# First mixer of a hybrid trunk on one Trainium2 core: S5 input and q/k products moved ahead of the output-gate tiles, pole exponentials packed, S5 output turned and transposed on TensorE, GLU first

## The reference, cut to what matters

```python
proj = xn @ w_in
u, xm, v, o_pre = jnp.split(proj, [512, 1024, 1536], axis=-1)
# S5: 32 groups x 16 channels, 64 complex states each
a_bar = jnp.exp(lam * dt)
b_bar = ((a_bar - 1.0) / lam)[..., None] * b
_, states = lax.associative_scan(_linear_recurrence_combine, (a_seq, bu), axis=1)
y = Re(C . states) + d_skip * u
g = jax.nn.gelu(y)
y_a = g * jax.nn.sigmoid(g @ w_glu)
# mLSTM: 4 heads of 128
xc = jax.nn.silu(causal_dwconv(xm, ml_conv_w, ml_conv_b))
q, k = per-head xc @ ml_w_q, xc @ ml_w_k
gates = concat(q, k, v) @ ml_w_gates + ml_b_gates
h_t = rmsnorm(mlstm_chunkwise(q, k, v, gates[..., :4], gates[..., 4:]))
y_b = jax.nn.sigmoid(o_pre) * h_t
return jnp.concatenate([y_a, y_b], axis=-1) @ w_out
```

## Time and profile before

| | us |
|---|---|
| median of 3 runs | 1192.64 (1188.93 to 1192.95) |
| the profiled execution, its own time | 1190.42 |
| its span, first to last instruction | 1188.2 |
| PE / DVE / ACT / POOL busy in the span | 1135.7 / 670.0 / 471.6 / 237.5 |
| mean granted TensorE clock | 0.971 |

### The profile page before, as it was taken

One profiled execution on the slowest core, in us unless ns is written; L12 is line 12 of the kernel. 1 busy time (PEld: TensorE's weight loads), 2 busy tenths in 40 slices (PEclk: granted clock), 3 DMA queues, 4 the chain that ended last, 5 costly groups with the idle time before them and its releaser, 6 DMA issues.

```text
span 1188.2 us, 15399 instructions
## 1 busy us (share of the span) xinstructions
PE 1135.7 (96%) x5386; PEld 909.4 (77%) x5386; DVE 670.0 (56%) x882; ACT 471.6 (40%) x675; POOL 237.5 (20%) x405
## 2 busy tenths in 40 slices
PE   8988779999999999999999999999999999999995
PEld 6876454877788888888888777777888888888883
DVE  5766765344766666664333566547666666652223
ACT  6324125353544344443222255535443443432221
POOL 8899797002000000000000012111000000000001
PEclk8999958899999999999999999999999999999998
DMA  6633001143223232323333321123323232223321
GB/s 225 128 105 105 1 1 58 36 142 106 88 90 106 88 104 90 105 89 106 106 101 102 104 75 54 38 71 107 106 88 106 88 106 88 98 97 107 106 71 71
DMA packets 39096, 108.77 MB, mean 92 GB/s; under 512 B 11984, under 2 KB 12240, under 8 KB 38928
## 3 DMA queue, kind: packets, MB, share of 16 engines
q1 hardware_dynamic: 39056, 108.24, 28.3%
HBM read 102.59 MB, written 4.19 MB: 90 GB/s over the span
## 4 chain that ended last, share of the span: by engine, by line
PE 83%; DVE 6%; POOL 5%; ACT 3%; issue 2%; DMA 1%; DVEq 0%; SPq 0%; ACTq 0%; POOLq 0%
PE bank L1289 24%; PE bank L1291 24%; PE bank L1290 24%; POOL ptmp L432 3%; PE bank L1540 1%; PE bank L1312 1%; PE bank L1385 1%; PE bank L1421 1%; ACT whi L604 1%; PE bank L1445 1%; PE bank L1426 1%; DVE wlo L879 1%; PE bank L1562 1%; PE bank L1446 1%; DMA raw<-wstream 1%
## 5 line engine op out<-in xcount | busy, mean ns | idle before, releaser
L1289 PE MATMUL bank<-xhi,whi 128*128 128x512 f32 x992 | 392.2, 395 | 14.7 <-DVE wlo L879 7.7
L1290 PE MATMUL bank<-xlo,whi 128*128 128x512 f32 x992 | 387.7, 391 | 0.0
L1291 PE MATMUL bank<-xhi,wlo 128*128 128x512 f32 x992 | 387.6, 391 | 0.0
L879 DVE TENSOR_TENSOR wlo<-raw,whi 128x1024 fp32r<-128x1024 f32 x181 | 227.4, 1257 | 276.2 <-ACT whi L604 275.4
L604 ACT ACTIVATE whi<-raw 128x1024 fp32r<-128x1024 f32 x181 | 191.1, 1058 | 370.8 <-PE bank L1291 346.1
L1289 PEld LDWEIGHTS bank<-xhi,whi 128*128 128x128 f32 x992 | 187.1, 189 | 59.9 <-DVE wlo L879 8.7
L1291 PEld LDWEIGHTS bank<-xhi,wlo 128*128 128x128 f32 x992 | 187.1, 189 | 39.5
L1290 PEld LDWEIGHTS bank<-xlo,whi 128*128 128x128 f32 x992 | 187.2, 189 | 38.7 <-issue 1.0
L1289 PE MATMUL bank<-ahi,whi 128*128 128x512 f32 x352 | 138.7, 394 | 0.0
L1291 PE MATMUL bank<-ahi,wlo 128*128 128x512 f32 x352 | 138.0, 392 | 0.0
L1290 PE MATMUL bank<-alo,whi 128*128 128x512 f32 x352 | 136.6, 388 | 0.0
(11 more groups left out here) (243 smaller groups left out, 1222.7 us busy)
## 6 DMA issues: line engine op xcount, KB each, us to landing
raw<-wstream SPq DMA_DIRECT2D x181, 512.0 KB, 3.3
xin<-xT SPq DMA_DIRECT2D x4, 512.0 KB, 7.2
h<-xT SPq DMA_DIRECT2D x1, 2048.0 KB, 7.7
outT<-outb SPq DMA_DIRECT2D x8, 256.0 KB, 2.2
u_scratch<-uperm SPq DMA_DIRECT2D x1, 1024.0 KB, 5.3
uc<-u_scratch SPq DMA_DIRECT2D x8, 128.0 KB, 5.9
y_scratch<-ysb SPq DMA_DIRECT2D x16, 64.0 KB, 2.2
uperm<-y_scratch SPq DMA_DIRECT2D x4, 256.0 KB, 2.8
```

The source lines that it names most:

```text
L879: V.tensor_tensor(wlo[:, t % RING, :], raw[:, t % RAWS, :], whi[:, t % RING, :].bitcast(f32), ALU.subtract).then_inc(lo_done, 1)
L1289: MM(dst, wh, rhi, start=start, stop=False)
L1290: MM(dst, wh, rlo, start=False, stop=False)
L1291: return MM(dst, wl, rhi, start=False, stop=stop)
```

## The change

- **Order of tiles.** T0 to T11 are u, xm, v; T12 is q/k; T13 to T16 the output gate (now between the stages of the serial part that follows: one behind q/k, one behind the forget rows, one behind K, one behind the transposes of K); T17, T18 GLU; T19, T20 YB; T21 on as before.
- **POOL.** Real and imaginary parts are packed in one 128 x 32 operand, so a squaring is five instructions instead of nine. The reciprocal of |lambda|^2 is asked for first. POOL makes steps 0 and 4 to 7 of `gg` (`gre` and `gim` in one tile); **DVE makes steps 1 to 3**, behind the work on tiles 7, 8 and 9. The transposes on PE wait for both (`g_built`, `g_mid`).
- **PE.** The S5 input product alternates even and odd groups; the twelve gate products go to four groups of 32 columns, and two products with `selg` add them up; K is made turned (32 stationary columns, 128 moving) in four column groups, copied by ACT to `kt` and transposed by PE.
- **Read-outs.** Steps 0 to 2 stand ahead of the heads, step 3 behind head 0's gate, 4 and 5 behind head 1's, 6 and 7 behind head 2's.
- **Heads** follow each other with no S5 output between them. One table set serves Exp and Ln (`preload_act_table_set`).
- **S5 output** behind the heads: `uc` and `xs` are stationary, `toep` and `ff` move; the result lies with chunks on the partitions, is copied to `ysb` and transposed by PE (16 transposes), and GELU reads PSUM. `y_scratch`, its 20 DMAs and `xdiag` are gone. The GLU weights and the first rows of `w_out` are permuted on the host to match.
- **End.** GLU first, then YB, then YA.

```diff
-T_IN, T_QK = 0, 16
-T_YB = 17
-T_GLU = 19
+T_IN, T_QK = 0, 12
+T_O = 13
+T_GLU = 17
+T_YB = 19
...
@@ SP
-        loads(10, T_QK)
...
+        for t in range(10, 20):
             load(t, t % RAWS, t - 1)
         sp.wait_ge(k_final, 1)
         sp.wait_ge(toep_clear, 1)
...
+        load(20, 0, 19)
+        load(21, 1, 20)
@@ DVE, input tiles
-        for t in range(16):
+        for t in range(12):
...
+            if t == 7:
+                dve.wait_ge(g0_done, 1)
+                dve.wait_ge(q_done, 1)
+            if 7 <= t < 10:
+                g_step(t - 6)
...
@@ DVE, between q/k and the heads
+        def out_gate(m):
+            wait_tile_used(dve, T_O + m)
+            V.tensor_tensor(sigo[:, m, :], bank[IN_BANK[O_O + m]][:, :], rstd[:, :], ALU.mult).then_inc(out_freed, 1)
+            split_lo(T_O + m + RING)
...
@@ DVE, heads
             head_gate(hd)
+            for step in ((3,), (4, 5), (6, 7), ())[hd]:
+                read_out(step)
@@ PE
-            for g in list(range(0, GROUPS, 2)) + list(range(1, GROUPS, 2)):
+            for g in range(GROUPS):
...
+            for j in range(4 * q, 4 * q + 4):
+                for f in range(2):
+                    MM(bank[q % 2][STATE * f:STATE * f + STATE, (j % 4) * P:(j % 4 + 1) * P], uc[:, 2 * j + f, :],
+                       toep[:, :, 2 * j + f, :], start=j == 4 * q, stop=False)
```

More of the change, by code:

```diff
@@ L337, in _ @@
         sp.dma_start(bcp[:, :, :], bc).then_inc(bc_in, 16)
-        loads(4, 10)
+        for t in range(4, 9):
+            load(t, t % RAWS, t - 1)
         sp.wait_ge(out_freed, 4)
         sp.dma_start(u_scratch.rearrange("m p s c -> p m (s c)"), uperm[:, :, :]).then_inc(u_saved, 16)
+        load(9, 1, 8)
         sp.wait_ge(u_saved, 16)
@@ L346, in _ @@
             sp.dma_start(uc[s * GCH:(s + 1) * GCH, :, :], src).then_inc(u_back, 16)
-        loads(10, T_QK)
-        load(T_QK, 0, T_QK - 1)
-        for t in range(T_QK + 1, T_YA + 1):
+        for t in range(10, 20):
             load(t, t % RAWS, t - 1)
@@ L371, in _ @@
         sp.dma_start(h[:, :, :], xT).then_inc(x_back, 16)
+        load(22, 0, 21)
         load(T_OUT, 1, T_OUT - 1)
@@ L521, in _ @@
+        pool.wait_ge(q_done, 1)
+        settle()
+        for s in range(4, CH):
+            g_step(s, gg[:, :, :, 0:GCH], qq[:, 0, s - 1, :], qq[:, 1, s - 1, :])
+        neg = bcp[:, 3, :]
+        G.tensor_scalar(neg, neg, -1.0, None, ALU.mult).then_inc(g_built, 1)
         pool.wait_ge(mean_done, 1)
```

580 lines of the change are left out of this document (320 added, 260 removed).

## The result

| | before | after |
|---|---|---|
| median | 1192.01 us (4 runs, 1188.93 to 1192.95) | 1169.84 us (4 runs, 1168.21 to 1172.1) |
| the profiled execution, its own time | 1190.42 | 1169.44 |
| its span | 1188.2 | 1167.6 |
| mean granted TensorE clock | 0.971 | 0.976 |

After takes 0.9816 of the time of before, 95% interval 0.98 to 0.9832: 22 us less. The prediction was 1170, with 1155 to 1184 as its range.

A forecast was written before the change was run, and what follows sets the result against it. PE was taken to bound the whole kernel, with waits in the first mixer's serial stretch; -19.6 - 3.1 + 3.2 + 13.9 - 10.2 - 4.5 = -20.3 from 1190.42 gave 1170.1, said as 1170, range 1155 to 1184.

The forecast's parts named there:

- Steps 1 and 3: Transposes start at 90.2, 19.6 us earlier, behind DVE's queue; S5 input takes 4.0 us, 3.1 less, by alternating column halves.
- Step 5: From q/k to the first head's product: 51.7 us, 3.2 more, through DVE's queue and T20's load behind `toep`.
- Step 6: The four heads: 53.5 us, 13.9 more, as DVE's read-outs stand ahead of weights PE waits for.
- Step 7: S5 output up to GLU: 15.1 us, 10.2 less, with quarters of 2.6 us.
- Step 8: GLU and YB: 21.8 us, 4.5 less, since YB covers PE's wait for the gate.
- DVE is not the bound: Rival in the heads and the stretch ahead: read-outs fall into DVE's idle time, heads take 40; 1150 to 1157, chance 0.2.
- DVE held by POOL everywhere: Rival in steps 1, 5 and 6: all read-outs at the price of 4.98 us; 1184, chance 0.2.
- Tiles don't overlap: Rival in S5 input, K and S5 output: each record on alternating tiles waits for the one before; 1249, chance 0.05.

The follow-up runs named there:

- e4_s5in_order: The changed kernel with S5 input's products back in blocks, all even groups and then all odd ones; 1173.74 us, ratio 0.9841 to the kernel before.
- e3_pool_steps: The changed kernel with two of DVE's three `g_step` given to POOL; 1172.51 us, ratio 0.9837 to the kernel before.
- e2_t20_first: The changed kernel with T20's load ahead of the eight `toep` transfers on SP instead of behind them; 1162.98 us, ratio 0.9764 to the kernel before.
- e1_reads_moved: The changed kernel with every read-out taken out of the heads to earlier places on DVE; 1155.87 us, ratio 0.9703 to the kernel before.
- e6_two_sets: The changed kernel without its requests for the joint ln and exp table set, so ACT changes sets again; 1170.33 us, ratio 0.9817 to the kernel before.
- e7_warm_pe: The changed kernel with 42 extra products in PE's idle time ahead of the transposes; 1169.85 us, ratio 0.9818 to the kernel before.

## Why the prediction was right, and where it was right by luck

**Steps 1 and 3: the mechanism right, the exact 90.2 partly luck.** The start at 90.23 is DVE's, `[6.79 <-DVE gg L944]`, with `g_built` done at 72.0, at the early edge of the predicted 72 to 85. The step's own sum was 80.5 + 11.2 = 91.7, and it took 90.2 with a reason that has no price in it. In the rows the convolution ended at 79.9 and the queue took 10.3: a `g_step` 2.2 to 2.5 instead of 2.45, a split and a read 1.74 instead of 1.95. But PE idled 6.8 us there, not 11: T11 ended at 83.4 instead of 79.1. The new table of banks puts T11 into the bank of T7, which DVE reads only at 74.01, behind T6's convolution (its three products took 4.05 us beside POOL's wide steps of g, which have moved forward to there; 3.17 before). PE waited 2.79 us for it (the row at 74.84) and then ran T11 at a mean clock of 0.65. It cost nothing, since the transposes waited for DVE longer still, but the step had looked at the end of DVE's queue and not at what else the new banks tie to it. S5 input at 4.0 rests on the pitch in the earlier trace rows; e4_s5in_order shows that order makes it, and e3_pool_steps that the same order takes 6.20 at a clock of 0.58. The step's 0.107 for a full array is not in the earlier trace rows, but other rows of before bear it out: a pair of 128 x 128 records took 0.38 (193.00), 0.11 from start to start at 0.27 each.

**Step 5: the mechanism right, two of its terms off in opposite directions.** Predicted 51.7, measured 50.0. From q/k to the last `toep` issue it had 42.3 and the rows 39.9. The three read-outs took 4.2, 3.4 and 3.8 up to the next instruction, not 5.0 each. The price was fair for before, where four in a row beside POOL took 4.65 to 5.15, but a read-out there was six instructions and is now four with the same elements, and POOL ran other work beside it; which of the two made the difference is not shown. Against that T20 landed in 4.8 instead of 3.3. (The step's additions slip by 0.3 to 0.4 in two places, 120.3 for 120.7 and 134.6 for 134.3, and nearly cancel.) The queue behind SP's `toep` transfers was found in the order and priced at 7.5; e2_t20_first gives 7.4.

**Step 6: right in sum, by luck, and in none of its three terms.** The prediction took heads of 42.3 without read-outs; e1_reads_moved shows 39.0. It priced the read-outs at 17.5; they took 12.1, as the last four ran after the scan, which ended at 182.6 as predicted, at 2.2 each. It subtracted a cover of 6.3; by PE's idle time it was 12.1 - 9.1 = 3.0. And it left out that PE's busy time itself grows by 5.4 when waits lower the clock, or rather it set it, unpriced, against the table loads, which brought nothing measurable in e6_two_sets. 42.3 + 17.5 - 6.3 = 53.5 and 39.0 + 12.1 - 3.0 + 5.4 = 53.5: four errors that cancel. The second sum only takes the measured 53.6 apart by e1_reads_moved and is no test of its own. The claim that DVE's place in the queue holds PE is shown; its numbers weren't known.

**Step 7: right.** Quarters of 2.9 instead of 2.6 (1.03 for the first kind, where 16 x 0.055 = 0.88, and 1.89 for the second, 32 x 0.055 = 1.76); 15.7 against 15.1.

**Step 8: the mechanism right, the term 1.0 too large.** GLU and YB run without a gap. But the 26.29 us of the earlier trace rows hold 102 records, and the stage has 96: six products of YA were in it, behind a wait of 1.54, and YA's own first wait of 1.05 ended it. Counted from YA's first product in both (266.46 and 247.4) the stage loses 1.9 and the stretch from YA on 1.6, together 3.5, which is the -4.5 and the +1.0 of the table.

**The rivals.** "DVE is not the bound" fell with the waits at all three changes of head. "DVE held by POOL everywhere" fell with the read-outs after the scan. "Tiles don't overlap" fell with the pitch. The Trainium skill's rule on modes (TensorEngine Tiling (Array Packing), Key Properties), by which a change of mode drains the array, would have added an estimated 3 to 4 us for some 14 changes. By the rows at 209.97 and 211.00 the 16 records of the first kind take 1.03 until the second begins, 0.15 more than their pitch; the 32 of the second take 1.89 (211.00 to 212.89) until the next mode, 0.13 more. Fourteen times 0.15 is about 2 us, an estimate. So the trace agrees with the rule in kind, as far as this excess is the drain, and shows about half of the price; it is what the quarters of 2.9 have over 2.6.

**What stays open.** How much of e2_t20_first's gain the scan takes back outside the profiled execution, since its median is 6.9 below after's and its profiled span only 4.0 (the profiled execution, 1165.4, was the slowest of its four); why the heads of one and the same code took from 51.1 to 54.2; and why T20's load took 4.8 us in some executions and over 6 in others. Giving the head's waits something useful to do on PE, as e7_warm_pe did for the transposes, wasn't tried.

## What to carry to other kernels

Price work that is inserted ahead of an in-order engine's critical instruction twice: for the wait and for the slower clock after it, here 9.1 and 5.4 us for 12.1 us of read-outs. Before taking a wait away, look who is second on the same boundary: moving two steps to POOL brought nothing (1172.5) until two splits moved as well (1162.9). And put filler work where its engine is idle and POOL is idle too; the same eight read-outs, rearranged, were worth 14 us.
